# Gated feed-forward blocks as seven quarter products, their weight sums made in DRAM

## The reference

```python
D_MODEL, SEQ, D_FF_2 = 1024, 512, 2816

def conv_ffn(h, p):
    a, b = jnp.split(h @ p["ffn_w_up"], 2, axis=-1)
    a = short_conv(a, p["ffn_conv_w"], p["ffn_conv_b"])
    return (jax.nn.gelu(a, approximate=False) * b) @ p["ffn_w_down"]

x = x + g_f * conv_ffn(modulate(rmsnorm(x, p["norm_ffn"]), sh_f, sc_f), p)
```

## Time and profile before

| | |
|---|---|
| median of 3 runs | 1446.36 us (1445.95 to 1446.55) |
| the profiled execution | 1446.32 us, of which the span is 1444.6 |
| TensorE busy | 1432.4 us, 99% of the span |
| VectorE, ScalarE, GpSimd busy | 866.6, 636.3, 381.0 us |
| chain that ended last | TensorE 94%, VectorE 3%, ScalarE 1% |
| granted TensorE clock | full (0.999 on average) |
| moved by DMA | 191 MB, 132 GB/s on average |

### The profile page before, as it was taken

The page is one execution under the profiler, slowest core; times in us unless marked ns, Lnnn a source line. Parts: engine busy times, 40 slices in busy tenths (PEclk is TensorE's granted clock), DMA queues, the critical chain, the costliest instruction groups (busy, mean ns, idle before and its releaser), DMA issues.

```text
span 1444.6 us, 18657 instructions
## 1 busy us (share of the span) xinstructions
PE 1432.4 (99%) x7320; PEld 1193.4 (83%) x7320; DVE 866.6 (60%) x1309; ACT 636.3 (44%) x1047; POOL 381.0 (26%) x327
## 2 busy tenths in 40 slices
PE   9999999999999999999999999999999999999998
PEld 6777778888878888888888888888889898889987
DVE  6455766444476644465448437788757976357744
ACT  6535773233453422344336336565445444234432
POOL 1263211102032200122013412116524541334302
PEclk9999999999999999999999999999999999999999
DMA  8351115654265544457436322234623224313331
GB/s 273 118 170 64 59 44 207 215 167 147 103 210 162 165 156 158 135 190 228 139 102 230 110 73 74 59 118 138 228 72 103 91 99 132 102 59 117 116 104 59
DMA packets 54913, 191.19 MB, mean 132 GB/s; under 512 B 6759, under 2 KB 7688, under 8 KB 54442
## 3 DMA queue, kind: packets, MB, share of 16 engines
q1 hardware_dynamic: 48314, 167.06, 35.3%
q0 software_dynamic: 4880, 17.30, 3.6%
q10 hardware_dynamic: 1632, 5.64, 1.1%
HBM read 177.38 MB, written 12.60 MB: 132 GB/s over the span
## 4 chain that ended last, share of the span: by engine, by line
PE 94%; DVE 3%; ACT 1%; issue 1%; DMA 0%; SPq 0%; POOL 0%; DVEq 0%; ACTq 0%
PE PS L613 92%; PE PS L626 2%; DVE TMP L2161 0%; DMA X<-in_x 0%; ACT wh L1416 0%; ACT HTh L1438 0%; DVE HTl L2129 0%; DVE TMP L2623 0%; DVE TMP L2584 0%; DVE wl L2111 0%; DVE TMP L2154 0%; ACT Y L1430 0%; ACT TMP L1514 0%; ACT TMP L1512 0%; DVE HTl L2376 0%
## 5 line engine op out<-in xcount | busy, mean ns | idle before, releaser
L2111 DVE TENSOR_TENSOR wl<-raw,wh 128x1024 fp32r<-128x1024 f32 x193 | 250.6, 1303 | 271.4 <-ACT wh L1416 270.9
L613 PE MATMUL PS<-HTh,wh 128*128 128x512 f32 (+1 forms) x1052 | 393.4, 375 | 1.0 <-DVE HTl L2129 0.9
L613 PE MATMUL PS<-HTl,wh 128*128 128x512 f32 (+1 forms) x1052 | 390.7, 373 | 0.0
L613 PE MATMUL PS<-HTh,wl 128*128 128x512 f32 (+1 forms) x1052 | 386.3, 372 | 0.0
L1416 ACT ACTIVATE wh<-raw 128x1024 fp32r<-128x1024 f32 x210 | 220.1, 1054 | 191.4 <-PE PS L613 183.2
L613 PEld LDWEIGHTS PS<-HTh,wh 128*128 128x128 f32 x1052 | 198.3, 189 | 41.9 <-issue 8.2
L613 PEld LDWEIGHTS PS<-HTl,wh 128*128 128x128 f32 x1052 | 198.4, 189 | 32.6 <-DVE HTl L2129 0.7
L613 PEld LDWEIGHTS PS<-HTh,wl 128*128 128x128 f32 x1052 | 196.1, 188 | 35.2 <-DVE wl L2111 0.2
L613 PE MATMUL PS<-wl,FFh 128*128 128x512 f32 (+1 forms) x442 | 169.9, 384 | 0.0
L613 PE MATMUL PS<-wh,FFh 128*128 128x512 f32 (+1 forms) x442 | 169.9, 384 | 0.0
L613 PE MATMUL PS<-wh,FFl 128*128 128x512 f32 (+1 forms) x442 | 169.8, 384 | 0.0
(11 more groups left out here) (373 smaller groups left out, 2460.3 us busy)
## 6 DMA issues: line engine op xcount, KB each, us to landing
raw<-in_ws SPq DMA_DIRECT2D x268, 512.0 KB, 4.1
taps<-TMP SPq DMA_DIRECT2D x16, 256.0 KB, 2.4
tab<-in_spec POOLq DMA_DIRECT2D x8, 512.0 KB, 5.8
raw<-taps SPq DMA_DIRECT2D x8, 512.0 KB, 3.8
kd<-TMP POOLq DMA_DIRECT2D x16, 256.0 KB, 6.6
wh<-in_wd POOLq DMA_DIRECT2D x8, 512.0 KB, 4.2
wl<-in_wd POOLq DMA_DIRECT2D x8, 512.0 KB, 5.6
kf<-kd SPq DMA_DIRECT2D x8, 512.0 KB, 4.5
```

What stands on the lines that cost most here:

```text
L613: return nc.tensor.matmul(out, l, r, start=start, stop=stop, skip_group_check=True)
L2111: tt(l, RAW[RAW_AT["unit", x, 0] % RAWS][:, :UNITS[x][2]], f32(h), ALU.subtract).then_inc(sem("lo_dve"), 1)
```

## The change

All blocks from the fifth on are computed with seven products. `sequence` writes their order as a pipeline: while block m begins, block m-1 ends. Two products' weights (128 x 512 each) form one unit ("duo"); the last duo of a run is used after the first unit of the down projection. The quarters are called a, b (gate, first and second half of the features), c, d (value), and the sums are ac, cd, acd and abcd. The sums of all blocks of a run are made in DRAM by 8 DMAs of GpSimd's queue, 4 plain and 4 accumulating (`sum_weights`), in 6 steps that GpSimd's program places between its other work, each waiting for the ones before; those of the second run partly in the first run's up stage, at blocks 5, 7 and 9. Five differences of activations are made instead of four sums and differences. Two of every seven duos are split by GpSimd, the others by VectorE. GpSimd's and ScalarE's special handling of the lower right quarter goes. In the second norm ScalarE's unit before tile 2 is left to the place before tile 4. SyncE loads the final norm's gain after the output projection instead of after the last up product. The input gets a copy of the up weights in quarters (`up4`), 32 rows of 2048 floats for each block and quarter.

```diff
+RUNS = (range(4, 12), range(12, 22))
+PLAIN, SUMMED = "abcd", ("ac", "cd", "acd", "abcd")
+def sequence(run):
+    out = [("cd", run[0]), ("acd", run[0]), ("d", run[0])]
+    for m in run[1:]:
+        out += [("abcd", m - 1), ("cd", m), ("a", m - 1), ("acd", m), ("d", m), ("b", m - 1), ("ac", m - 1)]
+    return out + [(f, run[-1]) for f in ("abcd", "a", "b", "ac")]
...
+    or u in DUOS and DUOS.index(u) % 7 in (2, 5))]
...
+            def times_cd(m):
                 for q in range(2):
+                    bank(("up", m, q), "uc_v", 7 * m + 6 + q)
+                product("cd", m, value_bank(m, LEFT_HALF), quarter(0, HALF(0)), True).then_inc(sem("p_part"), 1)
+            def times_acd(m):
+                product("acd", m, gate_bank(m, RIGHT_HALF), turned(0), True).then_inc(sem("p_part"), 1)
+            def times_d(m):
+                e.wait_ge(*COPIED("cd", m))
+                product("d", m, value_bank(m, LEFT_HALF), turned(1), False)
+            def times_abcd(m):
+                e.wait_ge(*ADDED("k", m))
+                product("abcd", m, gate_bank(m, LEFT_HALF), quarter(4, HALF(1)), True).then_inc(sem("p_part"), 1)
+            def times_a(m):
+                product("a", m, value_bank(m, RIGHT_HALF), turned(2), True).then_inc(sem("p_part"), 1)
+            def times_b(m):
+                e.wait_ge(*ADDED("c", m))
+                product("b", m, gate_bank(m, LEFT_HALF), turned(3), False).then_inc(sem("p_up"), 1)
+            def times_ac(m):
+                product("ac", m, value_bank(m, RIGHT_HALF), turned(4), False).then_inc(sem("p_up"), 1)
...
             for k in KT:
-                if k == 2:
-                    weights(u + 2 * SLOTS - 1)
                 if k == 4:
                     weights(unit("w_ff_in", 0, 0))
...
+                for m in run[1:]:
+                    weights(duo_ahead("abcd", m - 1))
+                    keep_abcd(m - 1)
+                    if m - 2 in run:
+                        gelu(m - 2)
+                    weights(duo_ahead("cd", m))
+                    keep_cd(m)
+                    if m - 2 in run:
+                        gated_high(m - 2, first_m)
+                    weights(duo_ahead("a", m - 1))
+                    weights(duo_ahead("acd", m))
+                    weights(duo_ahead("d", m))
+                    weights(duo_ahead("b", m - 1))
+                    centre(m - 1)
+                    weights(duo_ahead("ac", m - 1))
...
+                for m in run[1:]:
+                    if m - 2 in run:
+                        up_conv(m - 2)
+                    weights(duo_ahead("abcd", m - 1))
+                    gate_left(m - 1)
+                    if m - 2 in run:
+                        up_gate(m - 2)
+                    weights(duo_ahead("cd", m))
+                    weights(duo_ahead("a", m - 1))
+                    value_right(m - 1)
+                    gate_right(m - 1)
+                    weights(duo_ahead("acd", m))
+                    kernel_sum(m)
+                    weights(duo_ahead("d", m))
+                    weights(duo_ahead("b", m - 1))
+                    weights(duo_ahead("ac", m - 1))
...
+            def sum_weights(n, step):
+                rows = slice(32 * PAIRED.index(RUNS[n][0]), 32 * PAIRED.index(RUNS[n][-1]) + 32)
+                x = {f: a["up4"][i, rows, :] for i, f in enumerate(PLAIN)}
+                y = {f: a["sums"][i, rows, :] for i, f in enumerate(SUMMED)}
+                e.wait_ge("d_sum", 16 * (8 * n + (0, 2, 4, 5, 6, 7)[step]))
+                if step == 0:
+                    for f in ("ac", "cd"):
+                        engine.dma_start(y[f], x["c"], max_dma_last_dim=8192).then_inc(sem("d_sum"), 16)
+                elif step == 1:
+                    engine.dma_start(y["ac"], x["a"], accum_op=ALU.add, max_dma_last_dim=8192).then_inc(sem("d_sum"), 16)
+                    engine.dma_start(y["cd"], x["d"], accum_op=ALU.add, max_dma_last_dim=8192).then_inc(sem("d_sum"), 16)
...
+                for m in run[1:]:
+                    weights(duo_ahead("cd", m))
+                    if m - 2 in run:
+                        gated_low(m - 2, first_m)
+                    weights(duo_ahead("ac", m - 1))
+                    if m in (5, 7, 9):
+                        sum_weights(1, 3 + (5, 7, 9).index(m))
```

More of the change, by code:

```diff
@@ L190 @@
[L190 to L218, removed]
@@ L221 @@
[L221 to L245, removed]
@@ L246 @@
-APART = [j for j in range(NUSE) if USES[j][0] == "A22"]
+LANDED, _sum = [], [0] * RAWS
+for _n, (_kind, _x, _) in enumerate(LOADS):
+    _sum[_n % RAWS] += 32 if _kind == "unit" and _x in DUOS else 16
+    LANDED.append(_sum[_n % RAWS])
+OPERANDS = [x for run in RUNS for x in sequence(run)]
+PARTS = [x for x in OPERANDS if x[0] in ("cd", "acd", "abcd", "a")]
+COPIES = [x for x in OPERANDS if x[0] in ("cd", "abcd")]
+ADDS = [x for run in RUNS for m in [*run, run[-1] + 1]
+        for x in [(k, m - 1) for k in "guc" if m > run[0]] + [("k", m) for _ in range(m in run)]]
@@ L330, in highs @@
 def highs(u):
-    return u + 1 - sum(1 for v in PRE + APART if v <= u)
+    return u + 1 - sum(1 for v in PRE if v <= u)
 def mod_steps():
@@ L1389, in tensor_program @@
                     else:
-                        wide(*down)
+                        wide(*down, between=None if n else last_two)
         def scalar_program(engine):
@@ L2842, in vector_program @@
+                m = run[-1]
+                up_conv(m - 1)
+                weights(duo_ahead("abcd", m))
+                gate_left(m)
+                up_gate(m - 1)
+                value_right(m)
+                gate_right(m)
+                weights(unit("ffn_w_down_2", first_m * P, 0) + SLOTS - 1)
+                weights(duo_ahead("b", m))
                 up_conv(m)
@@ L2844, in vector_program @@
                 for n in range(2):
-                    weights(ahead_of(unit("ffn_w_down_2", (first_m + count - 1) * P, n * S)))
+                    weights(unit("ffn_w_down_2", (first_m + count - 1) * P, n * S) + SLOTS - 1)
                     for i in range(4):
@@ L3036, in gpsimd_program @@
                 tt(x, x, T(r % 2), ALU.add).then_inc(sem("rp_add"), 1)
-            weights(PRE[2])
+            sum_weights(0, 0)
+            mine = [u for u in range(PRE[2] + 1) if u > unit("w_in_2", 0, 0) and (u in POOL_LOW or u in PRE)]
+            for i, u in enumerate(mine):
+                weights(u)
+                if i in (0, 3, 5):
+                    sum_weights(0, (0, 3, 5).index(i) + 1)
+            sum_weights(0, 4)
             for o in range(2):
```

452 lines of the change are left out of this document (185 added, 267 removed).

## The result

The changed kernel takes 1484.84 us (median of 4 runs, 1482.21 to 1486.43), the one before 1446.15 (4 runs): the ratio is 1.0265, 95% interval 1.0248 to 1.0283. It is **slower by 38.7 us**; forecast were 4.4 us less. The profiled execution has a span of 1484.1 us.

The account below looks back on a forecast made before the run. TensorE, busy 1432.4 of 1444.6 us, was taken to bound the kernel. Columns -7.6, ScalarE's order +2.6, norm's order -0.4 and DMAs +1.0 make -4.4, so 1446.3 becomes 1441.9 us; range 1438.0 to 1449.0.

Parts of the forecast that it names:

- What bounds the kernel: Whole kernel: TensorE, busy 1432.4 of 1444.6 us; only fewer or shorter matmuls shorten the stretch from 1099.9 to 1432.9 us.
- Columns, -7.6 us: Nine block pairs in both runs: all-seven-product pairs take 20.16 us instead of 21.0, 0.84 saved each; bounds -7.3 and -7.8.
- Rival (d): Seven-product blocks: the columns bring nothing, short matmuls being held to another pace over long stretches; 1446 us, chance 0.03.
- ScalarE's order, +2.6 us, 0.37 us at seven blocks: Every second block: TensorE waits before d for ScalarE's copy of cd, behind a 7.4 us chain; bounds 0 to +7.
- The norm's order, -0.4: Second norm, before the third column tile: the first TensorE wait stays, the second shrinks; between -0.9 and +0.3 us.
- A sum packet of 0.6 us: Weight sums by DMA: an 8 KB packet takes 0.33 us if plain, between 0.33 and 0.66 if it accumulates.
- DMA contention, +1.0 us (0 to +5): Up stage: accumulating sums at blocks 5 and 9 put loads 10.1 us behind against a 9.2 us cushion, 0 to 2 each.
- The earlier ones lie where a unit lasts 5.4 us or more: Sums issued before the up stage: the same backlog is only half a cushion there, so they cost nothing.
- GpSimd late for its steps: Sum steps: GpSimd must find the previous step landed; 44 us available after 1072, 24 to 32 needed, so nothing.
- rival (c): Slower: accumulating packets over 0.9 us delay SyncE's loads at blocks 5 to 10 and GpSimd; 1453 us, chance 0.13.
- The first seven-product block, at nothing: Start of the first run: no cost was given to it; the queues were followed for one block m.
- The range's lower end: Whole kernel: 1438.0 us, from the better end of the copy-in-time rival with -7.8 and -0.9.

Follow-up runs that it names:

- experiment 13: Experiment 12 with VectorE's additions of partial products ahead of its splits, the only difference: 1438.43 us, ratio 0.9950.
- experiment 3: Changed kernel without the second run's four sums issued at blocks 1, 5, 7 and 9, loading plain quarters of the same size instead: 1463.01 us.
- experiment 2: Changed kernel with the two accumulating sums at blocks 5 and 9 made plain copies: 1470.98 us.
- experiment 6: Changed kernel with all sums issued early, the first run's from 504 us, the second's from 648 to 927 us: 1471.76 us.
- experiment 7: Changed kernel with all sums early, ScalarE's copies ahead of splits, and the second run's third unit split on VectorE instead of GpSimd: 1470.12 us, ratio 1.0165.
- experiment 10: Changed kernel with sums in 64 spaced pieces, ScalarE's copies and VectorE's additions ahead of splits, second run's third unit split on VectorE: 1458.59 us, ratio 1.0091.
- experiment 11: Experiment 10 with pieces before 960 us, GpSimd's first-run third-unit split ahead of its last gated low part, VectorE's additions restored except each run's first: 1442.67 us, ratio 0.9977.
- experiment 12: Experiment 11 with all units of the seven-product blocks split on VectorE, none on GpSimd: 1461.99 us, ratio 1.0115.

## Why the prediction was wrong

By its own steps:

- **What bounds the kernel**: right. TensorE alone did, and every loss is a wait of TensorE or the low clock behind one.
- **Columns, -7.6 us**: right. With all waits gone (experiment 13) the starts stay 0.120 us apart through both runs, and its trace gives the term itself: from the last addition to X to the end of the first run it is 3.4 us shorter than the kernel before, over the second run 4.2, together 7.6. Its median is 7.6 below too, but there the norm's 0.4 comes in and new small waits before 1100 us go against it (1.4 us in that trace). Rival (d) is refuted.
- **ScalarE's order, +2.6 us, 0.37 us at seven blocks**: the place was right (d of every second block, released by p1c), the size was 0.75 us in the full state of the pipeline, and it starts at 0.4. At the seven blocks together it is 5.1 us instead of 2.6 (2.1 in the first run of experiment 3, where no sum disturbs it, and 2.9 in the second). I took the undisturbed durations, since GpSimd's own split "of the block before ends about then". It doesn't: in the changed kernel both run at once,

```profile
1362.52 4.02 DVE L2043 TENSOR_TENSOR wl<-raw,wh 128x1024 fp32r<-128x1024 f32 x2 [1.46 <-ACT wh L1356]
```

  and two splits take 4.0 us instead of 2.4. The upper bound of 1.0 us named this. With 0.1 us for the first matmul behind each wait it is 0.85 us a pair: just what the columns save.
- **The norm's order, -0.4**: right, mechanism included. The waits of 0.56 and 0.30 us have become one, for GpSimd's low part as forecast, and the table's issue that TensorE releases comes at 738.96 us where it came at 739.32 (timeline of GpSimd).

```profile
406.55 4.76 POOL L2823 TENSOR_TENSOR wl<-raw,wh 128x1024 fp32r<-128x1024 f32 x2 [3.43 <-ACT wh L1356]
```

```profile
408.98 0.50 PE L536 MATMUL PS<-wh,tab 128*128 128x512 f32 x1 [0.72 <-POOL wl L2823]
```

- **A sum packet of 0.6 us**: right. 78.9% x 16 us x 16 / 333 = 0.61 us; plain ones take 0.315 (experiment 2). The Trainium skill's rule ("Collectives: The Full Stack", section "Part 3: Why 7× under link rate — side-by-side accounting") that a reducing DMA runs at about half a copy's rate agrees in the time of a packet. Beside loads the whole transfer is less than twice as long: it landed after 19.3 and 19.5 us, the plain ones of the same size after 12.1 and 13.3. That packets of the two rings alternate one for one was wrong: 706 load packets passed with 333 of the sum's.
- **DMA contention, +1.0 us (0 to +5): the step that failed.** The working had the loads 10.1 us behind after a sum and a cushion of 9.2 us or more. The measured shortfall is 16 x (179 - 81) / 179 = 8.8 us, even less than forecast. But the cushion is not there: loads issued 1 to 5 us after a sum landed 9 to 17 us later, most of them about when the sum did. In the first of the four waits TensorE lacked the split of a late unit. The other three, about 15 us, ended with ScalarE's copy, which stood in that engine's queue behind a late unit that TensorE uses three units later, with up to 6.7 us of helper work in a row between the landing and TensorE. I counted the depth of the buffers as time that TensorE can go on. I also took each sum by itself, while four follow one another 24 to 32 us apart. The waits are 17.7 us instead of 1, and the granted clock behind them, half for some 5 us after a wait of 9, adds a few. The plain sum at block 7, which I put at no cost, is 1.9 us of them; by the working's own rule it leaves loads 4.8 us behind, not 4.
- **"The earlier ones lie where a unit lasts 5.4 us or more": the second failure.** I weighed bytes on the shared engines, and not the order of GpSimd's own queue, on which tables that TensorE needs are issued right behind the sum. 12 us. Nor does "half a cushion" hold when sums follow without a pause (experiment 6).
- **GpSimd late for its steps**: it was not, in the sense of rival (c); but at the second run's start its additions to X (6.0 us) stand before a split that TensorE waits for, 2.5 us, which I had at nothing.
- **The first seven-product block, at nothing**: wrong. I followed the queues for a later block only. It waits 3.1 us whatever the sums do (experiment 3), and the chain that ends there shows the step: ScalarE's copy of cd(4) stands behind the convolution and gelu of block 3 and the high part of a unit.

```profile
1143.62 0.64 ACT TMP L1920
...
1145.54 1.04 ACT wh L1356
1146.58 0.28 ACT p1c L1940
1146.91 3.29 PE PS L536 x16
```

  VectorE's first addition and GpSimd's split of the third unit stand behind block 3's work in the same way: with the copy ahead TensorE waits for the addition (3.3 us, experiment 7), with the addition ahead too for that split (3.7 us, experiment 10), and with all three ahead, and ScalarE's high part of that unit with them, for nothing (experiment 11). The fifth shared difference, which I called hidden, has neither its high nor its low part in the chain above; its low part was moved in 10 and 11 together with the rest, so what it costs by itself was not separated.
- **The range's lower end**: its own terms, 1446.3 - 7.8 - 0.9, give 1437.6, not 1438.0.

Rival (c) had the right sign and place, loads at blocks 5 to 10, with a price (over 0.9 us a packet) that isn't what happened: its effect came at 0.61 us already. That experiment 11 measures 1442.67 us, close to the forecast of 1441.9, is luck: its queues have other orders than the change. The change as it stands with its sums out of the way would take about 1451 us, an estimate from experiment 3 (1463.0) less the 12 us of the table's wait.

## What to carry to other kernels

A bulk DMA beside a stream of loads is priced by how long one load's landing is delayed, and by what stands in order behind that landing, not by mean bandwidth against the depth of the buffers. Cut it into pieces that end sooner than the lead of the loads, pace them (both were done at once here), and look at what else its queue has to issue next. Before helper engines count as idle, write their queues out with the durations that they show when both work; and where TensorE waits for a short addition, put it ahead of the long work for later.

## What was not expected of the hardware

- After a wait of 8.9 us TensorE's granted clock was 0.50, the lower of its two levels (1.2 instead of 2.4 GHz), for about 5 us, and 0.87 in the 5 us behind: at half pace that is 2.5 us, and 0.13 x 5 = 0.7 behind it, so the wait costs a third more than its length. Shorter waits can do it too: behind one of 2.5 us the clock was 0.67 for 4.5 us, while behind waits of 1.95 us it stayed at 1.00 in one run of blocks and fell in the other (experiment 12).
- Where two rings have work, the packets of 8 KB took 79% of the DMA engines' time and 2 KB packets 23%, two small ones for each large one (experiment 3 shows what the loads take without the sum: 60%). Cutting the large ones to 2 KB gave the loads 33%.
- A VectorE subtraction of 128 x 1024 takes 1.21 to 1.23 us alone and up to 3.1 beside GpSimd's of the same shape (2.4 us). GpSimd's help is then worth nothing to VectorE: five cost it 5 x 1.87 = 9.3 us with it, seven 7 x 1.29 = 9.0 without (experiment 12) or 7 x 1.35 = 9.4 (experiment 13).
